# Storing a decoder layer's output from POOL in two indirect transfers that leave out the rows of the last expert

## The chip, the cores and the metric

The kernel runs on one core of one Trainium2 chip. The metric is the device time of one execution in microseconds; the median over several runs is compared.

## The reference

One layer of a decoder trunk on a sequence of T = 256 tokens of D = 2048 float32 values. A token mixer comes first (gMLP, with two large projections), and then a hierarchical mixture of 32 experts, of which every token takes two. The result is normed once more:

```
h = x + chunked_gmlp(rmsnorm(x, norm_mix), ...)
h = h + hier_moe(rmsnorm(h, norm_ffn), ...)      # 32 experts, top 2 of one group of 8
return rmsnorm(h, norm_final)                    # (1, 256, 2048) float32
# an expert: (silu(x @ w_gate) * (x @ w_up)) @ w_down, 2048 -> 512 -> 2048
```

Every expert's weights are three matrices of 4 MB, all of which are read from HBM, whichever tokens come to it.

## The kernel before

The tokens lie in two tiles of 128 (t = 0, 1) with the token on the partition. `acc[:, t, :]` holds the running sum of the layer, one row of 2048 floats (8 KB) per token.

**The experts.** Each expert works on at most CAP = 32 slots, that is on up to 32 tokens gathered by a matmul with a selection matrix. Then follow gate and up (L1564), a transpose of the result (L1641), down (L1662) and a scatter back to tokens (L1675) that DVE adds to `acc` (L1158). SyncE (SP) issues the loads of weights on its own queue, in the order of the experts, as soon as buffers are free. The last expert's down matrix comes in three transfers: the first half in one of 2 MB (L368), the second half in two of 1 MB (L479), each of one row of 8 KB per partition. The last four matmuls wait for the very last of them by `last_in`.

**The last expert is treated apart.** All 256 tokens are finished as if the last expert (number 31) did not exist, while its weights are still on their way. DVE adds expert 30 to `acc` (`add_before_last`, L1204 and L1208), ACT sums the squares (L824), and DVE multiplies by the norm in four instructions of 128x1024 (L1220), two per tile t, each counting up `out_ready`. SP then stores tile t in one transfer of 1 MB when `out_ready` has reached 2 (t + 1):

```
            for t in range(NT):
                sp.wait_ge(out_ready, 2 * (t + 1))
                sp.dma_start(out[0, t * P:(t + 1) * P, :], acc[:, t, :]).then_inc(out_stored, 16)
```

The rows of the last expert's 32 slots are made a second time. `place_tokens` computes for each token its slot (`place`, below 32 for those that have one). Tokens that were routed to expert 31 have their rank as slot, and the slots left over are filled with other tokens, so that exactly 32 tokens have a slot. PE gathers their row numbers (`slot_row`, L1699) and their rows of `acc` (L1704). After the last down matmul DVE adds the expert's output (L1301), ACT and PE make the sum of squares (L877, L1724), and DVE writes the normed rows (L1308, `rows_ready`). They lie as 128 pieces of 512 floats (4 quarters of 32 rows). POOL writes them over the rows stored before by one indirect transfer of 0.26 MB (L581). Since the same rows of `out` were already written by the bulk stores, POOL waits for these first:

```
            pool.wait_ge(slots_ready, 1)
            pool.wait_ge(rows_ready, 1)
            pool.wait_ge(out_stored, 16 * NT)
            pool.indirect_dma_start(...)
```

POOL's queue has other work before that: the loads of the mixer's norm rows (`g_ln`, `b_ln`, 8 KB per partition each) and, during expert 30, four loads of a piece of `norm_final` (L575). SP ends with waits on `out_stored` and `rows_stored`.

Of the kernel before, what the change touches and what calls it, by code (L numbers as in the profile page):

```python
# [10 lines left out]
ALU = mybir.AluOpType  # L11
# [3 lines left out]
P = 128  # L15
EPS = 1e-6
CAP = 32
# [3 lines left out]
def hybrid_layer(nc, x, norm_mix, norm_ffn, norm_final, w_in, ln_g, ln_b, w_s, b_s, w_out,  # L21
                 r_w_group, r_b_group, r_w_exp, r_b_exp, e_gate, e_up, e_down, out):
    _, T, D = x.shape
    NT = T // P
    KD = D // P
# [35 lines left out]
    with ExitStack() as ctx:  # L61
        def sem(name):
            return ctx.enter_context(nc.semaphore(name))

        def sb(name, shape, dt=F32, stack=ctx):
            return stack.enter_context(nc.sbuf_tensor(name, shape, dt))
# [59 lines left out]
        pass_e_i = sb("pass_e_i", [P, MAXX], I32)  # L126
        pass_rank = sb("pass_rank", [P, MAXX])
        pass_t = sb("pass_t", [P, MAXX])
# [15 lines left out]
        token, token_row, quarter = top[:, 0, 0:NT], top[:, 0, NT:2 * NT], top[:, 0, 4:5]  # L144
        place, place_free = top[:, 1, 0:NT], top[:, 1, NT:2 * NT]
        slot_row = pass_e_i[:, 0:1]

# [15 lines left out]
        acc = sb("acc", [P, NT, D])  # L165
# [17 lines left out]
        def xlo(k, n=1):  # L183
# [70 lines left out]
        ones_row_ready, g_ready, tokens_ready, out_ready = (  # L254
            sem("ones_row_ready"), sem("g_ready"), sem("tokens_ready"), sem("out_ready"))
        place_step, same_slot_ready, hot_ready, slots_ps, slots_ready = (
            sem("place_step"), sem("same_slot_ready"), sem("hot_ready"), sem("slots_ps"), sem("slots_ready"))
# [4 lines left out]
        rms_o_done, rstd_o_done, out_stored = sem("rms_o_done"), sem("rstd_o_done"), sem("out_stored")  # L262
# [63 lines left out]
        def chunk_at(i):  # L326
            return buffer_of(i), len(earlier[i])
# [32 lines left out]
        def _(sp):  # L360
# [106 lines left out]
            for e in range(LAST_LOOP, NEXP):  # L467
# [9 lines left out]
                else:  # L477
                    for b in range(2):
                        sp.dma_start(chunk_tile(i)[:, b, :], expert_chunk(i)[:, b, :]  # L479
                                     ).then_inc((chunk_in[chunk_at(i)[0]], last_in)[b], 16)  # L480
            for t in range(NT):
                sp.wait_ge(out_ready, 2 * (t + 1))
                sp.dma_start(out[0, t * P:(t + 1) * P, :], acc[:, t, :]).then_inc(out_stored, 16)
            sp.wait_ge(out_stored, 16 * NT)
            sp.wait_ge(rows_stored, 16)

# [2 lines left out]
        def _(pool):  # L489
# [84 lines left out]
            for j in range(NB):  # L574
                pool.dma_start(g_quarters[j * CAP:j * CAP + 1, :],  # L575
                               norm_final[j * NBLK:(j + 1) * NBLK].rearrange("(a n) -> a n", a=1)).then_inc(final_in, 16)

            pool.wait_ge(slots_ready, 1)
            pool.wait_ge(rows_ready, 1)
            pool.wait_ge(out_stored, 16 * NT)  # L580
            pool.indirect_dma_start(out[0].rearrange("t (j n) -> (t j) n", n=NBLK),  # L581
                                    bass.IndirectOffsetOnAxis(ap=slot_row, axis=0), slot_rows, None
                                    ).then_inc(rows_stored, 16)
# [299 lines left out]
        def _(dve):  # L883
# [276 lines left out]
            def expert(e):  # L1160
                if 0 < e < NEXP - 1:
                    add_out(e - 1, 0)
                if e == NEXP - 1:
                    dve.wait_ge(scatT_ready, NEXP)
                    add_before_last()
                make_hT(e)
                if e + 1 < NEXP:
                    scale_xeT(e + 1)
                if e + 2 < NEXP:
                    choose(e + 2)  # L1170
                if e == NEXP - 2:
                    place_tokens()
                    dve.wait_ge(scat_ps, NEXP)
                    for t in range(NT):
                        ins = dve.tensor_scalar(last_hot[:, t, :, :], iota_cap[:, :].unsqueeze(1).to_broadcast([P, NQ, CAP]),
                                                place[:, t:t + 1], None, ALU.is_equal)
                    ins.then_inc(hot_ready, 1)
                if 0 < e < NEXP - 1:
                    add_out(e - 1, 1)

            def place_tokens():
                rank = rank_of[:, :, NEXP - 1]
                dve.wait_ge(tokens_ready, 2 + NB)
                dve.scalar_tensor_tensor(out=place_free, in0=rank, scalar=-1.0, in1=token, op0=ALU.mult, op1=ALU.add
                                         ).then_inc(place_step, 1)
                dve.wait_ge(place_step, 1)
                dve.tensor_scalar(place_free, place_free, count_f[:, NEXP - 1:NEXP], 1000.0, ALU.add, ALU.add
                                  ).then_inc(place_step, 1)
                dve.wait_ge(place_step, 2)
                dve.tensor_tensor(place, place_free, rank, ALU.min).then_inc(place_step, 1)  # L1190
                dve.wait_ge(place_step, 3)

            def add_before_last():
                dve.wait_ge(gu_half, NEXP - 1)
                dve.tensor_reduce(fold, ident[:, :].rearrange("p (q c) -> p c q", q=NQ), AX_X, ALU.add).then_inc(place_step, 1)
                dve.wait_ge(place_step, 4)
                dve.tensor_copy(same_slot.rearrange("p (q c) -> p q c", q=NQ), fold.unsqueeze(1).to_broadcast([P, NQ, CAP])
                                ).then_inc(same_slot_ready, 1)
                dve.tensor_reduce(slot_weight, scatT[:, (NEXP - 1) % 2, :, :].rearrange("p t m -> p (t m)"), AX_X, ALU.add
                                  ).then_inc(weight_ready, 1)  # L1200
                for j in (2, 3):
                    dve.wait_ge(seed_ps, NB + j + 1)
                    cols = slice(j * NBLK, (j + 1) * NBLK)
                    dve.tensor_tensor(acc[:, 1, cols], FINAL[1][j][:, :], acc[:, 1, cols], ALU.add).then_inc(seed_done, 1)  # L1204
                for t, j, banks in SEEDED:
                    cols = slice(j * NBLK, (j + 2) * NBLK)
                    dve.wait_ge(seed_ps, NB * t + j + 2)
                    dve.tensor_tensor(acc[:, t, cols], banks, acc[:, t, cols], ALU.add).then_inc(seed_done, 1)  # L1208
                dve.wait_ge(slots_ps, 1)
                dve.tensor_tensor(slot_row, SLOT_ROW, quarter, ALU.add).then_inc(slots_ready, 1)  # L1210
                dve.wait_ge(slots_ps, 2)
                dve.tensor_copy(acc_slots, Y[:, :]).then_inc(slots_ready, 1)
                dve.wait_ge(rms_o_done, 1)
                dve.reciprocal(rstd_o, rms_o).then_inc(rstd_o_done, 1)
                dve.wait_ge(rstd_o_done, 1)
                dve.wait_ge(g_ready, 1)
                for t in range(NT):
                    for j in (0, 2):
                        cols = slice(j * NBLK, (j + 2) * NBLK)
                        dve.scalar_tensor_tensor(out=acc[:, t, cols], in0=acc[:, t, cols], scalar=rstd_o[:, t:t + 1],  # L1220
                                                 in1=G_FINAL[:, cols], op0=ALU.mult, op1=ALU.mult).then_inc(out_ready, 1)
# [629 lines left out]
```

## Time and profile before

| | |
|---|---|
| median of 3 runs | 1199.13 us (1198.53 to 1200.3) |
| the profiled execution | 1199.87 us, span 1198.1 us |
| PE busy, share of the span | 885.2 us, 74% |
| DVE / ACT / POOL busy | 380.9 / 232.1 / 23.0 us |
| HBM read / written | 458.05 MB / 2.36 MB, 384 GB/s over the span |
| chain that ended last | DMA 49%, PE 46% |

The span is the time between the first and the last instruction; the execution's own time has 1.8 us around it. The chain that ended last is followed back from the last instruction, at each step to what released it. The first quarter of the span is the mixer, in which PE is busy almost without a break; in the rest the 16 DMA engines are busy for over 90% of each slice, and move 423 to 434 GB/s until the last slice.

### The profile page before, as it was taken

To read this page: it belongs to the slowest core of one execution; us is meant where nothing else is said; L and a number is where in the kernel's file an instruction comes from. 1 tells how busy PE (TensorE), PEld (TensorE's weight loads), DVE (VectorE), ACT (ScalarE), POOL (GpSimd) and SP (SyncE) were. 2 spreads that over 40 slices of the span, in tenths; PEclk is the share of its full clock that TensorE was granted. 3 is DMA by queue.
4 is the path that set the end of the run, shared out by engine and by line. 5 is a ranking of instruction groups with operands and counts; after the bars stand their busy time and mean duration, and the time that the engine had idled before them with its cause. 6 is when DMAs were issued, how large, how long until landed. Compare 5 with 4: busy or idle time off the path is not lost.

```text
span 1198.1 us, 17564 instructions
## 1 busy us (share of the span) xinstructions
PE 885.2 (74%) x7809; PEld 502.3 (42%) x7809; DVE 380.9 (32%) x490; ACT 232.1 (19%) x390; POOL 23.0 (2%) x66
## 2 busy tenths in 40 slices
PE   9999999999984666666666666666666666666676
PEld 7788888877431222223232222322222222222232
DVE  5454866445232222222222222222222222222233
ACT  6544655434210000000000000000000000000003
POOL 1200000000200000000000000000000000000000
PEclk9999999999997777777787877878787878787788
DMA  8875567878999999999999999999999999999997
GB/s 278 321 262 188 190 229 250 298 265 306 396 423 434 428 432 432 429 433 433 429 433 433 430 432 433 430 432 432 430 433 432 430 433 430 433 430 432 427 427 337
DMA packets 47397, 460.93 MB, mean 385 GB/s; under 512 B 3992, under 2 KB 4608, under 8 KB 31744
## 3 DMA queue, kind: packets, MB, share of 16 engines
q1 hardware_dynamic: 46416, 457.19, 92.5%
q0 software_dynamic: 864, 3.21, 0.8%
q8 instruction: 24, 0.39, 0.1%
q14 instruction: 13, 0.11, 0.0%
q10 hardware_dynamic: 80, 0.02, 0.0%
HBM read 458.05 MB, written 2.36 MB: 384 GB/s over the span
## 4 chain that ended last, share of the span: by engine, by line
DMA 49%; PE 46%; ACT 2%; DVE 1%; SPq 1%; issue 1%; POOLq 0%; POOL 0%; ACTq 0%; DVEq 0%
DMA low_slots<-in_e_w_up 45%; PE scattered_out L1354 20%; PE bank L1564 13%; PE bank L1662 5%; PE pair L1525 3%; DMA high_slots<-in_e_w_up 2%; PE scattered_out L1675 1%; PE pair L1533 1%; DMA out_h<-acc 1%; DMA w_raw<-in_a_w_in 1%; ACT arena L776 1%; PE scattered_out L1316 0%; SPq L449 0%; DVE w_lo L889 0%; DVE acc L1220 0%
## 5 line engine op out<-in xcount | busy, mean ns | idle before, releaser
L1158 DVE TENSOR_TENSOR acc<-scattered_out,acc 128x2048 f32<-128x2048 f32 x58 | 132.9, 2291 | 617.4 <-PE scattered_out L1675 617.4
L1564 PE MATMUL bank<-low_slots,arena 128*32 128x256 f32 x2048 | 154.8, 458 | 146.4 <-DMA low_slots<-in_e_w_up 145.9
L1564 PE MATMUL bank<-high_slots,arena 128*32 128x256 f32 x1952 | 145.1, 454 | 137.7 <-DMA high_slots<-in_e_w_up 137.6
L1564 PEld LDWEIGHTS bank<-low_slots,arena 128*32 128x32 f32 x2048 | 83.1, 127 | 219.4 <-issue 188.9
L1564 PEld LDWEIGHTS bank<-high_slots,arena 128*32 128x32 f32 x1952 | 79.5, 126 | 204.6 <-issue 174.6
L889 DVE TENSOR_TENSOR w_lo<-w_raw,w_hi 128x1024 fp32r<-128x1024 f32 x95 | 116.4, 1225 | 114.6 <-ACT w_hi L597 114.1
L597 ACT CAST w_hi<-w_raw 128x1024 fp32r<-128x1024 f32 x95 | 100.2, 1054 | 127.1 <-PE scattered_out L1354 120.4
L1354 PE MATMUL scattered_out<-w_hi,xT_second 128*128 128x512 f32 x376 | 121.3, 394 | 0.2 <-DVE w_lo L889 0.2
L1354 PE MATMUL scattered_out<-w_hi,xT_first 128*128 128x512 f32 x376 | 120.4, 393 | 1.1 <-DVE w_lo L889 1.1
L792 ACT COPY arena<-bank 128x256 f32<-128x256 f32 x32 | 11.9, 373 | 546.2 <-PE bank L1564 546.2
L1662 PE MATMUL bank<-down_slots,arena 128*32 128x512 f32 x944 | 107.9, 595 | 2.1 <-DMA down_slots<-in_e_w_down 1.4
L1354 PEld LDWEIGHTS scattered_out<-w_hi,xT_first 128*128 128x128 f32 x376 | 70.6, 188 | 18.4 <-DVE w_lo L889 1.6
L1354 PEld LDWEIGHTS scattered_out<-w_hi,xT_second 128*128 128x128 f32 x376 | 70.6, 188 | 17.8 <-DVE w_lo L889 0.9
L1354 PE MATMUL scattered_out<-w_lo,xT_second 128*128 128x512 f32 x188 | 73.5, 391 | 0.0
L1354 PE MATMUL scattered_out<-w_lo,xT_first 128*128 128x512 f32 x188 | 73.4, 390 | 0.0
L1675 PE MATMUL scattered_out<-arena 32*128 32x512 f32 x480 | 68.4, 640 | 0.0
L1525 PE MATMUL pair<-h,arena 128*32 128x512 f32 x496 | 59.7, 598 | 0.0
L1662 PEld LDWEIGHTS bank<-down_slots,arena 128*32 128x32 f32 x944 | 27.3, 109 | 60.3 <-issue 56.5
L803 ACT COPY arena<-bank 128x512 f32<-128x512 f32 x31 | 18.2, 587 | 170.1 <-PE scattered_out L1675 162.5
L1354 PEld LDWEIGHTS scattered_out<-w_lo,xT_second 128*128 128x128 f32 x188 | 35.4, 188 | 6.3
L1354 PEld LDWEIGHTS scattered_out<-w_lo,xT_first 128*128 128x128 f32 x188 | 35.3, 188 | 6.1
L1675 PEld LDWEIGHTS scattered_out<-arena 32*128 32x128 f32 x480 | 18.7, 182 | 37.5 <-issue 37.5
(271 smaller groups left out, 514.9 us busy)
## 6 DMA issues: line engine op xcount, KB each, us to landing
down_slots<-in_e_w_down SPq DMA_DIRECT2D x26, 4096.0 KB, 21.1
low_slots<-in_e_w_gate SPq DMA_DIRECT2D x13, 4096.0 KB, 30.5
low_slots<-in_e_w_up SPq DMA_DIRECT2D x13, 4096.0 KB, 39.4
high_slots<-in_e_w_gate SPq DMA_DIRECT2D x13, 4096.0 KB, 30.5
high_slots<-in_e_w_up SPq DMA_DIRECT2D x13, 4096.0 KB, 39.7
w_raw<-in_a_w_in SPq DMA_DIRECT2D x64, 512.0 KB, 3.7
w_raw<-in_a_w_out SPq DMA_DIRECT2D x32, 512.0 KB, 4.8
down_slots<-in_e_w_down SPq DMA_DIRECT2D x6, 2048.0 KB, 18.9
```

Source lines behind the costliest of these rows:

```text
L597: act.copy(w_hi[:, hc % 2, :, :], w_raw[:, hc % 4, :, :]).then_inc(hi_done, 1)
L776: act.copy(xe, XE[:, :]).then_inc(xe_ready, 1)
L792: act.copy(gu, GU[:, 0:256]).then_inc(gu_ready, 1)
L803: act.copy(y_sb, Y[:, :]).then_inc(y_ready, 1)
L889: dve.tensor_tensor(w_lo[:, hc % 2, :, :], w_raw[:, hc % 4, :, :], w_hi[:, hc % 2, :, :].bitcast(F32), ALU.subtract).then_inc(lo_done, 1)
L1158: dve.tensor_tensor(acc[:, t, :], OUT[:, :], (acc if e else h)[:, t, :], ALU.add).then_inc(acc_done, 1)
L1354: ins = pe.matmul(Z[parity][t][:, :], a(k)[:, toks], b[:, hc % 2, j, :], start=(k == 0 and part == 0), stop=(k == KD - 1 and part == 2))
L1525: ins = pe.matmul(XE[j * CAP:(j + 1) * CAP, :], sel[:, e % 2, t, :], gather_columns(t, j), start=(t == 0), stop=(t == NT - 1))
L1533: ins = pe.transpose(TRX[:, b * P:(b + 1) * P], xe.rearrange("p (c k) -> p k c", k=KC)[:, b, :], ident[:, :])
L1564: ins = pe.matmul(GU[c * CAP:(c + 1) * CAP, 0:256], rows_k, gate_columns(rows_of[c // 2][k], c % 2), start=(a == 0 and k == 0), stop=(a == ...
L1662: ins = pe.matmul(Y[j * CAP:(j + 1) * CAP, :], hT[:, b, c * CAP:(c + 1) * CAP], tile[b][:, j * NBLK:(j + 1) * NBLK], start=(c == 0 and b = ...
L1675: ins = pe.matmul(O[j], scatT[rows_j, e % 2, t, :], y_sb[rows_j, :], start=True, stop=True)
```

## The change

The two bulk stores go from SP to POOL and become indirect transfers: each row of `acc` goes to the row number in `kept_row[:, t]`. DVE makes these numbers in `place_tokens` with two more instructions on 128x2 elements: `in_slot` is 512 for a token that has a slot and 0 otherwise, and `kept_row = in_slot + token`. A number above T - 1 = 255 is out of bounds, and the row is left out, without an error. So the bulk stores write 224 rows and the slot rows' transfer the other 32. No row is written twice, and the slot rows' transfer does not wait for `out_stored` any more. `pass_e_i` and `pass_t`, in which the numbers lie, are lists for the extra passes, whose work is over by then.

```diff
+        kept_row, in_slot = pass_e_i[:, 2:2 + NT], pass_t[:, 0:NT]
...
-            for t in range(NT):
-                sp.wait_ge(out_ready, 2 * (t + 1))
-                sp.dma_start(out[0, t * P:(t + 1) * P, :], acc[:, t, :]).then_inc(out_stored, 16)
             sp.wait_ge(out_stored, 16 * NT)
             sp.wait_ge(rows_stored, 16)
...
+            pool.wait_ge(place_step, 5)
+            for t in range(NT):
+                pool.wait_ge(out_ready, 2 * (t + 1))
+                pool.indirect_dma_start(out[0], bass.IndirectOffsetOnAxis(ap=kept_row[:, t:t + 1], axis=0), acc[:, t, :], None,
+                                        bounds_check=T - 1, oob_is_err=False).then_inc(out_stored, 16)
+
             pool.wait_ge(slots_ready, 1)
             pool.wait_ge(rows_ready, 1)
-            pool.wait_ge(out_stored, 16 * NT)
             pool.indirect_dma_start(out[0].rearrange("t (j n) -> (t j) n", n=NBLK),
...
                 dve.wait_ge(place_step, 3)
+                dve.tensor_scalar(in_slot, place, float(CAP), float(2 * T), ALU.is_lt, ALU.mult).then_inc(place_step, 1)
+                dve.wait_ge(place_step, 4)
+                dve.tensor_tensor(kept_row, in_slot, token, ALU.add).then_inc(place_step, 1)
...
-                dve.wait_ge(place_step, 4)
+                dve.wait_ge(place_step, 6)
```

The end of SP's program before (`down_slots` holds the last down matrix, `out_h` is the output in HBM):

```order
138 L368 DMA down_slots<-in_e_w_down 128x4096 [waits y_half]
139 L479 DMA down_slots<-in_e_w_down 128x2048 [waits y_ps]
140 L479 DMA down_slots<-in_e_w_down 128x2048
141 L483 DMA out_h<-acc 128x2048 [waits out_ready] x2
142 L61 UNCONDITIONAL_BRANCH [waits rows_stored,out_stored]
```

With the change the row with L483 is gone from SP, and nothing else on it has moved. The end of POOL's program before:

```order
60 L573 MEMSET low_slots 128x128 [waits gu_half,tokens_ready]
61 L575 DMA low_slots<-in_norm_final 1x16x32 x4
62 L581 DMA out_h<-arena,pass_e_i 1024x512 [waits out_stored,rows_ready,slots_ready]
63 L61 UNCONDITIONAL_BRANCH
```

and with the change:

```order
60 L571 MEMSET low_slots 128x128 [waits gu_half,tokens_ready]
61 L573 DMA low_slots<-in_norm_final 1x16x32 x4
62 L579 DMA out_h<-acc,pass_e_i 256x2048 [waits out_ready,place_step]
63 L579 DMA out_h<-acc,pass_e_i 256x2048 [waits out_ready]
64 L584 DMA out_h<-arena,pass_e_i 1024x512 [waits rows_ready,slots_ready]
65 L61 UNCONDITIONAL_BRANCH
```

The two stores stand on POOL between the loads of `norm_final` and the slot rows' transfer, which has lost its wait on `out_stored`. On DVE, at the end of expert 30, with the change (`arena` is here `last_hot`, the slots' one-hot matrices):

```order
429 L1193 TENSOR_TENSOR top<-top,rank_of 128x2 [waits place_step]
430 L1195 TENSOR_SCALAR pass_t<-top 128x2 [waits place_step]
431 L1197 TENSOR_TENSOR pass_e_i<-pass_t,top 128x2 [waits place_step]
432 L1178 TENSOR_SCALAR arena<-iota_cap,top 128x128 [waits scat_ps]
433 L1178 TENSOR_SCALAR arena<-iota_cap,top 128x128
434 L1161 TENSOR_TENSOR acc<-scattered_out,acc 128x2048 [waits scattered]
```

The second and third of these are new, and stand ahead of `last_hot` and of the add of expert 29's second tile.

## Rows read from the trace of the kernel before

**Rows 1.** The chain of waits in its last 17 us: start, duration, what
```profile
1181.70 11.92 DMA out_h<-acc
...
1194.27 1.31 POOLq L61
```

**Rows 2.** Timeline, 1160 to 1198 us: start, duration, instruction, idle before it
```profile
1160.59 0.23 DVE L1187 TENSOR_SCALAR top<-top,count_f 128x2 f32<-128x2 f32 x1
1160.85 0.16 DVE L1190 TENSOR_TENSOR top<-top,rank_of 128x2 f32<-128x2 f32 x1
...
1161.44 2.28 DVE L1158 TENSOR_TENSOR acc<-scattered_out,acc 128x2048 f32<-128x2048 f32 x1
...
1165.41 0.70 PE L1688 MATMUL pair<-arena 32*128 32x512 f32 x2 [0.80 <-ACT arena L803]
...
1167.49 1.29 DVE L1204 TENSOR_TENSOR acc<-bank,acc 128x512 f32<-128x512 f32 x2 [2.89 <-PE bank L1688]
...
1176.81 4.86 DVE L1220 SCALAR_TENSOR_TENSOR acc<-acc,rows,scattered_out 128x1024 f32<-128x1024 f32 x4
...
1179.32 2.73 SPq L483 DMA_DIRECT2D out_h<-acc  x2
...
1188.75 1.07 PE L1662 MATMUL bank<-down_slots,arena 128*32 128x512 f32 x8 [1.37 <-DMA down_slots<-in_e_w_down]
...
1191.54 0.56 PE L1724 MATMUL pair<-v_mean_var,low_slots 128*128 128x1 f32 x2 [1.72 <-ACT low_slots L877]
...
1192.63 0.75 DVE L1308 SCALAR_TENSOR_TENSOR arena<-arena,v_stats,pair 128x512 f32<-128x512 f32 x1
1194.52 1.07 POOL L581 DMA_INDIRECT out_h<-arena,pass_e_i  x1 [48.15 <-DMA out_h<-acc]
```

**Rows 3.** DMA queues, 1182 to 1188 us: packets, MB, share of the 16 engines
```profile
q1 hardware_dynamic: 336, 2.51, 100.3%
```

**Rows 4.** DMA queues, 1150 to 1151 us, while the norm_final loads run
```profile
q1 hardware_dynamic: 30, 0.43, 99.7%
q0 software_dynamic: 30, 0.00, 2.0%
```

**Rows 5.** DMA queues, 34 to 39 us, while g_ln and b_ln load
```profile
q0 software_dynamic: 230, 1.75, 84.9%
q1 hardware_dynamic: 153, 0.28, 15.7%
```

**Rows 6.** POOL's issue of the norm_final loads, and its queue from 1148 to 1150 us
```profile
1144.28 2.09 POOL L575 DMA_DIRECT2D low_slots<-in_norm_final  x4 [0.28 <-issue]
...
q0 software_dynamic: 55, 0.00, 2.0%
```

**Rows 7.** DMA queue and issue of the slot rows' transfer, 1194 to 1198.1 us
```profile
q0 software_dynamic: 80, 0.26, 15.7%
...
out_h<-arena,pass_e_i POOLq DMA_INDIRECT x1, 2.8
```

**Rows 8.** Windows: PE, PEld, DVE, ACT, POOL busy; granted clock, DMA share, GB/s
```profile
1188.00:1190.00 2.00, 1.07 (x8) 0.16 (x8) 0.11 (x1) 0.00 (x0) 0.00 (x0) 1.00 0.95 401
1190.00:1191.00 1.00, 0.00 (x0) 0.00 (x0) 0.64 (x1) 0.33 (x1) 0.00 (x0) 1.00 0.76 320
1191.00:1192.00 1.00, 0.46 (x2) 0.49 (x2) 0.00 (x0) 0.40 (x2) 0.00 (x0) 0.58 0.49 205
...
1194.00:1196.00 2.00, 0.00 (x0) 0.00 (x0) 0.00 (x0) 0.00 (x0) 1.07 (x1) 0.50 0.00 0
1196.00:1198.10 2.10, 0.00 (x0) 0.00 (x0) 0.00 (x0) 0.00 (x0) 0.00 (x0) 0.50 0.31 125
```

**Rows 9.** The gate and up matmuls (L1564) alone, in two windows
```profile
1120.30:1125.60 5.30, 5.29 (x52) 2.80 (x56) 0.50 0.99 427
1169.20:1173.00 3.80, 3.78 (x64) 2.35 (x64) 1.00 0.99 423
```

## The prediction

> **What bounds the kernel now.** I read the chain of waits first, from its end. It ends in DMA out_h<-acc, from 1181.70 to 1193.62 us, and then in POOL's last transfer [rows 1]. So the removed wait is the one that decides, and the change aims at the right place. The question is what stands behind it. The timeline tells: DVE finishes the slot rows (L1308) at 1192.63 + 0.75 = 1193.38 us, only 0.24 us before the stores have landed [rows 1, 2]. And that second path starts from another transfer: the last eight down matmuls (L1662) begin at 1188.75 us, when the last piece of the down matrix has come in [rows 2]. From there the path is a plain chain of PE, DVE and ACT to 1193.38, which takes 4.63 us.
>
> The third view is the DMA queues. From 1182 to 1188 us SP's queue (q1) alone keeps the 16 engines at 100.3% [rows 3]. There is no free bandwidth before 1188 us, so each byte that is stored earlier pushes a byte of weights back. SP issues its stores from 1179.32 us on, 9.4 us before the last weights are used, but behind them on the same queue. The last weights land at about 1188.73 us and the second store 4.89 us later, at 1193.62 [rows 1, 2]. That is what 2 MB at some 430 GB/s take: the stores come after the weights, on the slowest of the 16 engines at least, and cost them next to nothing. This order is what the change gives up.
>
> **The change, step by step.**
>
> 1. The wait on the stores goes. With the slot rows ready at 1193.38 in place of 1193.62 the end moves by **-0.24 us**. All that follows the release stays: 0.90 us until POOL begins [1193.62 to 1194.52, rows 1, 2], 1.07 us for the instruction, 2.8 us from issue to landing [rows 7], to the span's end at 1198.1. This is the whole gain that there is to have. It holds as long as the slot rows are not late.
>
> 2. DVE gets two instructions on 128x2 elements, 0.23 + 0.16 = 0.39 us by their neighbours L1187 and L1190 [rows 2]. Behind them stands the add of expert 29 (L1158), which ends at 1163.72; PE's next user of it (L1688) starts at 1165.41 and is released by ACT. 1.7 us are free, and DVE then sits idle for 2.89 us before L1204 [rows 2]. Cost 0; without that cover it would be 0.39 us. `last_hot`, made right after them, is used over 10 us later.
>
> 3. SP loses two issues, behind which nothing stands but the final waits: 0.
>
> 4. POOL gets two issues. The first is released when DVE's second L1220 ends, at 1176.81 + 4.86 / 2 = 1179.24 us, and the second at 1181.67 [rows 2]. Each takes 1.07 us if 128 rows cost what 128 pieces cost in L581. The trace has no indirect transfer with rows of 8 KB; the bounds are 1.07 us (price per row) and 4 x 1.07 = 4.3 us (price per byte). I take 1.07, since both have 128 rows. By either, POOL is free at 1190 us at the latest, before the slot rows need it.
>
> 5. **The stores move to another queue, and this is what costs.** When does their first packet move? The slot rows' transfer began at 1194.52, and no byte moved before 1196 [rows 2, 8]: at least 1.5 us. The norm_final loads, on engines full of weights, were issued from 1144.28 and have their first packets between 1148 and 1150 [rows 6]: at least 3.7 us. The first store is issued at 1179.24 + 0.90 = 1180.14, so its first packet moves between 1181.6 and 1183.9 us. At that time the slowest engine has 7.1 to 4.8 us of weights left (to 1188.73).
>
>    Does POOL's queue wait behind SP's? No: from 1150 to 1151 us, with q1 at 99.7%, q1 moves 30 packets and q0 30 [rows 4]. The engines take the queues in turn, packet by packet. The same shows in the bytes from 34 to 39 us: q0 with rows of 8 KB has 84.9% of the engines and q1 15.7% [rows 5]. The weights to come (two transfers of 1 MB with rows of 8 KB) have packets as large as the stores', so in turns the stores get half. An engine has 16 store packets in 4.89 us (2 MB over 16 engines in rows of 8 KB), 0.31 us each. Of these 1 in 8 falls away (32 of 256 rows), which leaves 14. With 4.8 us of weights left, or 15 packets, all 14 store packets still get a turn ahead of the last weight packet. So the last weights come later by 4.89 x 7/8 = **+4.28 us**. The bounds are 0 (q0 served last, or too late) and 4.89 (no row of the slowest engine left out). I take 4.28, because both bounds of the start lead to it.
>
>    On the packets' size, rows 5 have 1.75 MB in 230 packets, 7.6 KB on average with the small ones among them, so an 8 KB row goes as one packet. The Trainium skill, "DMA: Bandwidth & Descriptors", section "SWDGE vs HWDGE vs iDMA", says that a packet should rather have at most 4096 B. By the trace the sum below is 5.1 us, by that rule 3.5 us (third rival).
>
> 6. **PE's clock.** The last 8 matmuls take 1.07 us at a granted clock of 1.00, that is 2.4 GHz [rows 2, 8]. But the clock falls to 0.5 (1.2 GHz) between 1191 and 1192 us, after a stretch in which PE had little to do but these eight [rows 8]. With the change the last piece comes at about 1193.0 and the one before it about 3 us later than now, so PE has the same little bursts with longer gaps, and the last eight run after the fall. L1564 takes 5.29 / 52 = 0.102 us per matmul at 0.50 and 3.78 / 64 = 0.059 at 1.00 [rows 9], a factor of 1.7; the bound by the clock is 2. At 2 the eight take 2.14, at 1.7 1.84. I take **+1.07 us**, since these matmuls have no other wait among them; the other end is 0, where the clock holds on. L1724 at 1191.54 ran at the lower clock already, so it costs nothing more.
>
> Sum: -0.24 + 4.28 + 1.07 = +5.11 us. Against the profiled execution (1199.87 us) that gives 1204.98. It was 0.74 us above the median of the runs, 1199.13; the forecast goes by the median: **1204.2 us**.
>
> **The rivals.**
>
> First rival, not slower: the stores do not push the weights back. That takes a first packet on the slowest engine after 1188.73, or a queue q0 that only gets what q1 leaves. The stores then land about 4.3 us later, at 1193.0, the slot rows are ready at 1193.38, and the end moves by -0.24: 1198.9 us, which is within the 0.2% (2.4 us) that a measurement of this kernel can tell from no change. For it: SP's own stores now do just that, with no loss. Against it: rows 4 and 5 show turns, and POOL would have to be late by 8.6 us after 1180.14, where 3.7 us are the most that I found. It decides from a delay of 5.5 us on: then 3.1 us of weights are left, half of which is a term of 1.6, and the sum is under 2.4 us. I give it 0.12.
>
> Second rival: POOL's issue goes by bytes, 4.3 us each. The first store is then ready at 1184.4 and the second at 1188.7, and only the first one's 7 packets have a turn before the weights end: -0.24 + 2.14 + 1.07 = +3.0, that is 1202.1 us. Against it, 128 rows each. Chance 0.06.
>
> Third rival: the stores go in packets of 4 KB. Rows 7 have 0.26 MB in 80 packets, 16 of them for the semaphore, so 4 KB each; but there two pieces of 2 KB are in a packet, and rows 5 speak against a limit. Each turn would then give 0.155 us to the stores against 0.31 us to the weights. In 4.8 to 7.1 us of weights, the earliest in larger packets, there are 15 to 19 turns, 2.4 to 3.0 us: -0.24 + 2.7 + 1.07 = +3.5, that is 1202.7 us. The rest of the stores lands behind the weights but ahead of the slot rows. The Trainium skill's sentence above is this rule. Chance 0.15.
>
> Fourth rival: the row numbers do not take effect, or out-of-bounds rows cost an engine as much as others. Then the term is 4.89: 1204.8 us, inside the forecast's own range.
>
> A gain of more than 2.4 us would need weights that come earlier than now, and nothing in the change does that. I leave 0.02 for what I do not see.
>
> **How the numbers follow.** The forecast with its own bounds (clock held or not, 14 or 16 packets: +4.0 to +5.7, and half a microsecond around it) has 0.65, from 1202.6 to 1205.4. The second and third rival have 0.21, the first 0.12, the unseen gain 0.02. Slower by over 0.2%: 0.65 + 0.21 is 0.86, less 0.02 for a partial delay under 2.4 us, 0.84. Within 0.2%: 0.14. Faster: 0.02. The range takes in the second and third rival and ends below at 1200.9, short of the first; above it goes to 1206.0, for a POOL that is a microsecond late at the end.
>
> **What the changed profile would show.** Two store issues on POOL at about 1180.1 and 1182.6, of 1.1 us each. From 1182 to 1192 us q0 and q1 with a similar number of packets each. The last eight down matmuls at about 1193.0 in place of 1188.75, at a granted clock of 0.5, taking about 2 us. L1308 ending at about 1198.7, and POOL's last transfer released by it, with the chain of waits going through the last down load and no longer through out_h<-acc. If instead those matmuls still start near 1188.8, step 5 is wrong; if they start between 1190.5 and 1192, the turns are unequal (third rival) or POOL was late (second). If they take 1.07 us, step 6 is wrong.

## The result, and the profile after

| | before | changed |
|---|---|---|
| median | 1198.99 us (12 runs, 1197.95 to 1200.3) | 1202.33 us (12 runs, 1200.62 to 1203.74) |
| ratio | | 1.0028, 95% interval 1.002 to 1.0035 |
| profiled execution | 1199.87 us, span 1198.1 us | 1202.47 us, span 1200.7 us |

The changed kernel is 3.3 us slower: a small difference, but clear of the noise. The forecast was 5.1 us slower, 1204.2 us, with a range from 1200.9 to 1206.0.

The chain of waits of the changed kernel, at its end, tells what took the place of the wait that went (start, duration, what; to compare with [rows 1]):

```profile
1165.26 25.57 DMA down_slots<-in_e_w_down
1190.83 0.04 issue
1190.87 1.98 PE bank L1668 x8
...
1195.62 0.76 DVE arena L1314
...
1196.92 1.19 POOLq L61
```

It no longer goes through out_h<-acc but through the last load of the down matrix, which lands at 1190.83 us. Before, its matmuls began at 1188.75 [rows 2]. The timeline of the changed kernel over the same stretch (lines have moved by three to six, L1564 is now L1570, L1662 is L1668, L1308 is L1314):

```profile
1161.27 0.17 DVE L1195 TENSOR_SCALAR pass_t<-top 128x2 f32<-128x2 f32 x1
...
1161.47 0.16 DVE L1197 TENSOR_TENSOR pass_e_i<-pass_t,top 128x2 int32<-128x2 f32 x1
...
1165.63 0.70 PE L1694 MATMUL pair<-arena 32*128 32x512 f32 x2 [0.80 <-ACT arena L806]
...
1177.03 4.86 DVE L1226 SCALAR_TENSOR_TENSOR acc<-acc,rows,scattered_out 128x1024 f32<-128x1024 f32 x4
...
1178.39 3.84 PE L1570 MATMUL bank<-high_slots,arena 128*32 128x256 f32 x64
1180.46 1.11 POOL L579 DMA_INDIRECT out_h<-acc,pass_e_i  x1 [34.81 <-DVE acc L1226]
...
1182.69 0.99 POOL L579 DMA_INDIRECT out_h<-acc,pass_e_i  x1 [1.12 <-DVE acc L1226]
...
1186.28 1.07 PE L1668 MATMUL bank<-down_slots,arena 128*32 128x512 f32 x8 [0.43 <-DMA down_slots<-in_e_w_down]
...
1190.87 1.94 PE L1668 MATMUL bank<-down_slots,arena 128*32 128x512 f32 x8 [3.53 <-DMA down_slots<-in_e_w_down]
...
1195.62 0.75 DVE L1314 SCALAR_TENSOR_TENSOR arena<-arena,v_stats,pair 128x512 f32<-128x512 f32 x1
1197.14 0.97 POOL L584 DMA_INDIRECT out_h<-arena,pass_e_i  x1 [13.45 <-DVE arena L1314]
```

Three things are to be seen. POOL issues the stores at 1180.46 and 1182.69, 1.11 and 0.99 us each. The last eight down matmuls start at 1190.87 and take 1.94 us in place of 1.07. The last transfer is released by DVE's L1314, as was meant.

For the shift of the weights a measure is needed that does not move when a whole execution is half a microsecond earlier or later at this place. I take the distance from the end of the last gate and up matmul to the start of the last eight down matmuls. Before it is 1188.75 - (1179.02 + 3.89) = 5.84 us, with the matmuls of L1564 from the timeline of before:

```profile
1179.02 3.89 PE L1564 MATMUL bank<-high_slots,arena 128*32 128x256 f32 x64
```

With the change it is 1190.87 - (1178.39 + 3.84) = 8.64 us: the weights are **2.80 us** later. With the 0.87 us of the slower matmuls and -0.24 us for the wait that is gone that makes 3.43 us, and the medians differ by 3.34. (The two profiled spans differ by only 2.6 us, since in the changed kernel's execution the gate and up product ended 0.68 us earlier, and POOL's last transfer began 0.77 us after its release and took 0.97 us, where it was 0.90 and 1.07 us before.)

The DMA queues of the changed kernel, one line per queue (packets, MB, share of the 16 engines), from 1182 to 1184.3 us:

```profile
q1 hardware_dynamic: 124, 0.93, 97.6%
```

and from 1184.3 to 1185:

```profile
DMA packets 51, 0.29 MB, mean 421 GB/s; under 512 B 15, under 2 KB 15, under 8 KB 15
...
q1 hardware_dynamic: 24, 0.15, 50.8%
q0 software_dynamic: 27, 0.15, 50.7%
```

Up to 1184.3 us POOL's queue (q0) moves nothing, though its first store was issued at 1180.46. Then the two share the engines by halves at once, packet for packet. Of the 51 packets 15 are under 512 B; the other 36 carry the 0.29 MB, 8 KB each, and both queues moved 0.15 MB, so the stores' packets are as large as the weights'. The stores do not slow a packet down either: in the trace a weight packet of 8 KB takes 0.31 us (median) before the first store packet and after it.

One more view is needed further on, the queues from 1190.1 to 1190.8 us:

```profile
q0 software_dynamic: 17, 0.13, 44.2%
q1 hardware_dynamic: 1, 0.00, 0.1%
```

The weights' queue carries no row any more, but one small packet, and yet the last eight matmuls start only at 1190.87 us. The trace has the last weight packet's end at 1190.03: from there to the matmuls are 0.84 us.

### The profile page after: what moved, and what is told of

Its sections match the earlier page's. It is cut to its first block, busy times and chain, and to the rows that moved or that the text cites. A ratio compares the mean times of both kernels' runs of the same rounds, so it can differ in the third digit from the quotient of the medians.

```text
span 1200.7 us, 17568 instructions
## 1 busy us (share of the span) xinstructions
PE 886.9 (74%) x7809; PEld 502.3 (42%) x7809; DVE 381.4 (32%) x492; ACT 231.5 (19%) x390; POOL 25.0 (2%) x68
## 4 chain that ended last, share of the span: by engine, by line
DMA 50%; PE 46%; ACT 1%; SPq 1%; DVE 1%; issue 1%; POOLq 0%; ACTq 0%; DVEq 0%
DMA low_slots<-in_e_w_up 45%; PE scattered_out L1360 20%; PE bank L1570 13%; PE bank L1668 5%; PE pair L1531 3%; DMA high_slots<-in_e_w_up 2%; DMA down_slots<-in_e_w_down 2%; PE scattered_out L1681 1%; PE pair L1539 1%; DMA w_raw<-in_a_w_in 1%; ACT arena L779 1%; SPq L450 0%; SPq L466 0%; DMA arena<-in_a_b_s 0%; DVE w_lo L892 0%
## 5 line engine op out<-in xcount | busy, mean ns | idle before, releaser
L1570 PE MATMUL bank<-low_slots,arena 128*32 128x256 f32 x2048 | 154.7, 458 | 145.2 <-DMA low_slots<-in_e_w_up 144.7
L1570 PE MATMUL bank<-high_slots,arena 128*32 128x256 f32 x1952 | 146.1, 456 | 137.8 <-DMA high_slots<-in_e_w_up 137.7
L1570 PEld LDWEIGHTS bank<-low_slots,arena 128*32 128x32 f32 x2048 | 84.3, 127 | 217.1 <-issue 187.4
L1570 PEld LDWEIGHTS bank<-high_slots,arena 128*32 128x32 f32 x1952 | 79.0, 126 | 207.0 <-issue 176.5
L1668 PE MATMUL bank<-down_slots,arena 128*32 128x512 f32 x944 | 109.0, 599 | 4.7 <-DMA down_slots<-in_e_w_down 4.0
L1668 PEld LDWEIGHTS bank<-down_slots,arena 128*32 128x32 f32 x944 | 27.3, 110 | 63.2 <-issue 56.5
```

Source lines behind the costliest of these rows:

```text
L1570: ins = pe.matmul(GU[c * CAP:(c + 1) * CAP, 0:256], rows_k, gate_columns(rows_of[c // 2][k], c % 2), start=(a == 0 and k == 0), stop=(a == ...
L1668: ins = pe.matmul(Y[j * CAP:(j + 1) * CAP, :], hT[:, b, c * CAP:(c + 1) * CAP], tile[b][:, j * NBLK:(j + 1) * NBLK], start=(c == 0 and b = ...
```

## The experiments

All times are compared with runs of the kernel before on the same chip. "Shift" is the distance just defined, less the 5.84 us of before.

**Queue or form: plain stores from POOL.** The kernel before, with this edit:

```diff
-            for t in range(NT):
-                sp.wait_ge(out_ready, 2 * (t + 1))
-                sp.dma_start(out[0, t * P:(t + 1) * P, :], acc[:, t, :]).then_inc(out_stored, 16)
...
+            for t in range(NT):
+                pool.wait_ge(out_ready, 2 * (t + 1))
+                pool.dma_start(out[0, t * P:(t + 1) * P, :], acc[:, t, :]).then_inc(out_stored, 16)
             pool.wait_ge(slots_ready, 1)
```

> Kernel before, but POOL issues the two 1 MB stores as plain transfers of all 256 rows; the slot rows' transfer still waits for them. If the queue is the cost (POOL's queue takes turns with the weights'), the last eight down matmuls start 2 to 3.5 us later than before and the time is 3 to 5 us above before, as with the change or a little more, since no row is left out. If the indirect form or its bounds check is the cost, the time is that of before, within 1 us.

Measured: 1203.74 us against 1198.54, ratio 1.0044 (1.003 to 1.0058). From its timeline:

```profile
1177.33 3.83 PE L1564 MATMUL bank<-high_slots,arena 128*32 128x256 f32 x64
1177.92 0.56 POOL L577 DMA_DIRECT2D out_h<-acc  x1 [33.23 <-DVE acc L1220]
...
1191.97 1.94 PE L1662 MATMUL bank<-down_slots,arena 128*32 128x512 f32 x8 [3.84 <-DMA down_slots<-in_e_w_down]
```

The shift is 1191.97 - 1181.16 - 5.84 = 4.97 us, more than expected, and 4.89 us is what 2 MB take. The cost is the queue, and not the time of the issue: SP issued the same stores at 1179.32 us, 3.6 us before the end of the gate and up matmuls, and POOL 3.2 us before it. The indirect form is not needed for the cost, and is the milder one. Why milder, the last experiments tell.

**The wait alone.** The kernel before, without the wait, and with the slot rows in a DRAM tensor of their own, so that nothing is written twice (the 32 rows of the output stay without the last expert):

```diff
-            pool.wait_ge(out_stored, 16 * NT)
-            pool.indirect_dma_start(out[0].rearrange("t (j n) -> (t j) n", n=NBLK),
+            pool.indirect_dma_start(slot_out[0].rearrange("t (j n) -> (t j) n", n=NBLK),
```

> Kernel before, but the slot rows go to a DRAM tensor of their own and their transfer no longer waits for the stores, which stay on SP's queue (so 32 rows of the output keep the values without the last expert). This is the removal of the wait alone. My theory: 0.2 to 0.3 us less than before, below what can be measured; last eight down matmuls still at about 1188.7 us. A rival in which the wait was worth more than the two paths' difference: over 1 us less.

Measured: 1198.18 us against 1198.54, ratio 1.0 (0.9991 to 1.0009), shift 0.05 us. The best that removing the wait can give is below what can be measured, since the slot rows are ready just when the stores land.

**Holding the stores back.** The changed kernel, with one wait ahead of the two stores on POOL, in one run for the last gate and up product, in the other for the first half of the last down product:

```diff
             pool.wait_ge(place_step, 5)
+            pool.wait_ge(gu_ps, NEXP)        # in the other run: pool.wait_ge(y_half, NEXP)
             for t in range(NT):
```

> The changed kernel, with POOL's stores held until the last gate and up matmul (about 1182.3 us in place of 1179.5). Theory of turns: the first store packet moves about 1186.5 us, with at most 2 us of weights left on the slowest engine, so the down matmuls start 0.5 to 1 us later than before; with the clock term (0 to 0.9 us) the time is 0.3 to 1.7 us above before. Rival, a fixed price of POOL's indirect stores: still 3.3 us above before.

> The changed kernel, with POOL's stores held until the first half of the last down product (about 1185.9 us). Theory of turns: first store packet at about 1189 us, after the last weights, which come as before (1188.7); the stores land by about 1194 and the slot rows go right behind them: between 0.3 us less and 0.5 us more than before. Rival of a fixed price: 3.3 us above before.

Measured: 1198.52 us for the first, ratio 0.9999 (0.999 to 1.0008), and 1198.16 for the second, ratio 0.9997 (0.9988 to 1.0006), against 1198.54. Each has the same two stores, the same bounds check and the same missing wait as the changed kernel; only the start differs. From the timeline of the first:

```profile
1178.85 3.86 PE L1571 MATMUL bank<-high_slots,arena 128*32 128x256 f32 x64
1183.70 1.11 POOL L580 DMA_INDIRECT out_h<-acc,pass_e_i  x1 [37.44 <-PE bank L1571]
...
1188.98 1.07 PE L1669 MATMUL bank<-down_slots,arena 128*32 128x512 f32 x8 [1.79 <-DMA down_slots<-in_e_w_down]
```

and of the second:

```profile
1177.68 3.85 PE L1571 MATMUL bank<-high_slots,arena 128*32 128x256 f32 x64
...
1186.14 1.11 POOL L580 DMA_INDIRECT out_h<-acc,pass_e_i  x1 [41.01 <-PE bank L1669]
1187.42 1.06 PE L1669 MATMUL bank<-down_slots,arena 128*32 128x512 f32 x8 [1.40 <-DMA down_slots<-in_e_w_down]
```

The shifts are 0.43 and 0.05 us, and the last eight matmuls take 1.07 us again. This settles the fixed price: there is none that can be measured. The first of the two came out below what I expected (0.5 to 1 us of shift, 0.3 to 1.7 us of time): stores issued 3 us later cost nothing measurable. Its first store packet moved at 1185.40 us, when weights were still on their way, but the slowest engine can have served only one or two store packets (0.43 us) ahead of its last weights.

**The clock.** The changed kernel, with ten matmuls on constants, into a bank that is free by then, ahead of the wait for the last piece:

```diff
                         if i == NCHUNK - 1 and b == 1:
+                            keep_busy(10, GU)
                             pe.wait_ge(last_in, 32)
```

> The changed kernel with ten bf16 matmuls on constants into a free PSUM bank ahead of PE's wait for the last piece of the down matrix. If the clock is a term of its own, it stays at 1.00 through the last eight down matmuls, which take 1.07 us in place of 1.94, and the time is about 0.9 us under the changed kernel, that is 2.4 us above before. If the clock stays at 0.5 or the term is hidden, no difference from the changed kernel (3.3 above before).

Measured: 1201.65 us against 1198.83, ratio 1.0022 (1.0011 to 1.0032). The two windows of the down matmuls alone (PE busy, PEld busy, granted clock, DMA share, GB/s), first of the changed kernel, for the third and for the last group of eight:

```profile
1186.00:1187.40 1.40, 1.07 (x8) 0.16 (x8) 1.00 1.00 421
1190.80:1192.90 2.10, 1.94 (x8) 0.20 (x8) 0.50 0.18 74
```

and of this experiment:

```profile
1185.90:1187.10 1.20, 1.06 (x8) 0.16 (x8) 1.00 1.00 423
1190.80:1191.90 1.10, 1.07 (x8) 0.16 (x8) 1.00 0.06 22
```

The clock of the last eight is 0.50 (1.2 GHz) with the change, after PE had been idle for 3.53 us before them, and 1.00 (2.4 GHz) where the ten matmuls ran in that gap. The term is 1.94 - 1.07 = 0.87 us, as the trace shows directly. The medians agree in sign (2.8 us above before in place of 3.3, where I expected 2.4), but their intervals overlap, so by time alone it is not shown. This run's shift was 3.67 us, against 2.80, so that not all of the 0.87 shows in the time.

**The wait put back.** The changed kernel with `pool.wait_ge(out_stored, 16 * NT)` restored ahead of the slot rows' transfer.

> The changed kernel with POOL's wait on the stores restored ahead of the slot rows' transfer. The stores have landed by 1192 us and the slot rows are ready at 1196.4, so my theory says: the same as the changed kernel, 3.3 us above before. If the removed wait gave anything back, this one is slower still.

Measured: 1202.07 us, ratio 1.0028 (1.0019 to 1.0037), the same as the changed kernel. The removed wait gave nothing back, for with the change the stores land well before the slot rows are ready. In its profiled execution the last eight matmuls took 1.53 us, at a granted clock of 0.81 at first and of 0.50 then, so the clock's term is not the same 0.87 us in every execution.

**Rows left out or not.** The same, and the factor `float(2 * T)` in `in_slot` is 0.0, so that the indirect stores write all 256 rows, before the slot rows' transfer goes over 32 of them.

> As wait_back, but kept_row is the token's own number for all, so the indirect stores leave out no row (the factor in in_slot is 0). It lies between the changed kernel and the plain stores from POOL: 16 packets on each engine in place of 14, but a start as late as the indirect form's. If the late start limits the shift, the last down matmuls start about as in the changed kernel (2.8 to 3.5 us later than before, by the distance from the last gate and up matmul) and the time is 3.3 to 4 us above before. If the left out rows were what made the shift smaller than 4.9, it is as with the plain stores: 5 us later, and 5 us above before.

Measured: 1202.61 us against 1198.83, ratio 1.0029 (1.002 to 1.0039), shift 1191.71 - 1182.15 - 5.84 = 3.72 us:

```profile
1178.31 3.84 PE L1571 MATMUL bank<-high_slots,arena 128*32 128x256 f32 x64
1179.61 1.11 POOL L579 DMA_INDIRECT out_h<-acc,pass_e_i  x1 [34.13 <-DVE acc L1227]
...
1191.71 1.93 PE L1669 MATMUL bank<-down_slots,arena 128*32 128x512 f32 x8 [3.82 <-DMA down_slots<-in_e_w_down]
```

With all rows stored, the shift is still 1.25 us less than with plain stores. So the left out rows are not the main reason why it is smaller than 4.9. They may be a part: the shift is 0.72 us more than with the wait put back, where the stores were issued 0.4 us later, and a little above the 3.5 that I expected at most; the ratio does not tell the three kernels apart. What a left out row costs the engines can be read from POOL's queue, in the changed kernel from 1182 to 1193 us, and then in this one from 1183.8 to 1192.6:

```profile
q0 software_dynamic: 288, 1.84, 39.7%
```

```profile
q0 software_dynamic: 288, 2.10, 56.4%
```

The number of packets is the same, but 0.26 MB are missing, 32 rows of 8 KB. In the trace each left out row is a packet of 4 B that takes 9 ns.

**One store.** The changed kernel, with tile 0 stored by SP as before, and POOL's last transfer waiting for that one:

```diff
-            for t in range(NT):
+            for t in range(1, NT):
                 pool.wait_ge(out_ready, 2 * (t + 1))
...
+            sp.wait_ge(out_ready, 2)
+            sp.dma_start(out[0, 0:P, :], acc[:, 0, :]).then_inc(x_in[0], 16)
```

> The changed kernel with tile 0 stored by SP as before (POOL's last transfer waits for that store), and only tile 1 by POOL. Its release is 2.4 us later than that of the changed kernel's first store, so by the theory of turns its first packet moves at about 1186.7 us with 1.4 us of weights left on the slowest engine: a shift of 0 to 1.4 us, and 0 to 1.5 us above before (tile 0 may end the chain again). Rival, a price per indirect store: half of 3.3, 1.7 us above before, or more.

Measured: 1199.65 us against 1198.83, ratio 1.0006 (0.9997 to 1.0015), shift 1.11 us:

```profile
1167.80 5.48 PE L1574 MATMUL bank<-high_slots,arena 128*32 128x256 f32 x64 [2.12 <-DMA high_slots<-in_e_w_up]
...
1179.06 3.83 PE L1574 MATMUL bank<-high_slots,arena 128*32 128x256 f32 x64
...
1189.84 1.06 PE L1672 MATMUL bank<-down_slots,arena 128*32 128x512 f32 x8 [2.49 <-DMA down_slots<-in_e_w_down]
```

By the medians this is less than half of the change's 3.4 us, but the interval reaches 1.8 us, so that this run alone does not exclude 1.7 us per store; the two kernels that hold both stores back do. The shift is uncertain here too. The last expert's first gate and up matmuls took 5.48 us, and before 3.83:

```profile
1169.22 3.83 PE L1564 MATMUL bank<-high_slots,arena 128*32 128x256 f32 x64 [1.81 <-DMA high_slots<-in_e_w_up]
```

Counted from the start of this group, which waits for the last load of the up matrix, the last eight down matmuls begin 1189.84 - 1167.80 = 22.04 us later, against 1188.75 - 1169.22 = 19.53 before: a shift of 2.51 us, as much as all of tile 1's packets take on an engine (8 of 0.31 us). In each other run whose group waits for that load the two measures agree within 0.1 us. How much one store costs stays open between 1.11 and 2.51 us in this execution; the time of the median says 0.7.

**Plain stores, later.** The plain stores from POOL once more, but the first one waits for three of DVE's four instructions in place of two (`out_ready` 3).

> As pool_plain (plain stores of all rows from POOL, wait kept), but the first store waits for three of DVE's four instructions in place of two, 1.2 us later, which is about by how much the indirect form's first packet comes later than the plain one's. If the shift is the number of store packets that still get a turn ahead of the last weight packet, the shift falls from 4.97 us to between 3.5 and 4.2 us, like all_rows, and the time is 3.5 to 4.5 us above before in place of 5.2. If the shift is simply the 2 MB, it stays at 4.9.

Measured: 1202.58 us against 1198.83, ratio 1.0025 (1.0014 to 1.0036):

```profile
1178.05 3.86 PE L1564 MATMUL bank<-high_slots,arena 128*32 128x256 f32 x64
1180.60 0.56 POOL L577 DMA_DIRECT2D out_h<-acc  x1 [35.19 <-DVE acc L1220]
...
1190.89 1.94 PE L1662 MATMUL bank<-down_slots,arena 128*32 128x512 f32 x8 [3.82 <-DMA down_slots<-in_e_w_down]
```

The shift is 1190.89 - 1181.91 - 5.84 = 3.14 us, 1.8 us less than for the same stores issued earlier, and somewhat below the 3.5 that I expected at least. In this execution the issue was 1.9 us later against the gate and up product, not 1.2, which fits. All runs with stores on POOL, in the order of the first store's issue:

| kernel | first issue on POOL, us before the last gate and up matmul's end | shift of the last weights, us | time above before, by ratio, us |
|---|---|---|---|
| plain | 3.24 | 4.97 | 5.3 |
| changed, PE kept busy | 2.73 | 3.67 | 2.6 |
| all rows | 2.54 | 3.72 | 3.5 |
| wait put back | 2.14 | 3.00 | 3.4 |
| changed | 1.77 | 2.80 | 3.4 |
| plain, later | 1.31 | 3.14 | 3.0 |
| one store (tile 1) | 0.19 | 1.11 (or 2.51, see above) | 0.7 |
| held to the gate and up product | -0.99 | 0.43 | -0.1 |
| held to the half down product | -4.61 | 0.05 | -0.4 |

(The first two columns come from one execution each, the last from the medians of many.) Apart from the one store, the shift falls with a later start over the whole range, and neither the form of the transfer nor the 32 rows moves a kernel off this trend by more than about half a microsecond.

## Why the prediction was right, and where it was too high

The measured 1202.33 us lies in the stated range, but just below the 1202.6 to 1205.4 to which the forecast's own mechanism was given 0.65. It was caught by the part that was added for the second and third rival, neither of which holds. So the direction and the mechanism are to the prediction's credit, and the hit is in part luck of a wide range. One of its own signs came true as well: the last matmuls started at 1190.87, between 1190.5 and 1192, where it blamed unequal turns or a late POOL. Neither was so, the turns are equal and POOL's instructions took 1.11 and 0.99 us. The stores' first packet was late.

- **Step 1, the wait** (-0.24): right. Alone it is worth nothing that can be measured, and the chain of waits changed hands as described. That all behind the release stays was not quite so: POOL's start and instruction took 0.23 us less.
- **Steps 2 to 4** (nothing): right. DVE's two instructions took 0.17 and 0.16 us, PE's L1694 is still released by ACT (0.80 us, as in [rows 2]), and POOL takes 1.11 and 0.99 us per store, which is the price per row (1.07) and not per byte (4.3). The second rival falls with it.
- **Step 5, the stores push the weights back** (+4.28): the mechanism is right, with turns of one packet each, q0 and q1 at 50.7% and 50.8%. The size was too high: 2.80 us. The sentence that failed is "With 4.8 us of weights left, or 15 packets, all 14 store packets still get a turn". I put the first store packet between 1181.6 and 1183.9 us. It moved at 1184.3, because the indirect store was released at 1179.46 and issued at 1180.46, 1.00 us later and not 0.90, and its first packet came 3.8 us after that, hardly less than the norm_final loads' [rows 6] and far from the idle engines' 1.5. In this execution the last weights would have been used at 1182.23 + 5.84 = 1188.07. So some 3.8 us were left and not 4.8 to 7.1, which would be 12 packets of 0.31 us each. But this counts, as the prediction did, the weights up to the matmuls' start, and the last weight packet ends before it: 0.84 us in the changed kernel, and 0.53 us in the one held to the half down product (1186.89 to 1187.42). That leaves 2.9 to 3.2 us of packets, 9 or 10. The shift of 2.80 us is 9 of them, one store packet for each weight packet that was left. This is an estimate, for the views do not name the single engine, and the first store packet on the slowest may come after the first on any. That the plain stores, issued 1.5 us earlier against the weights, cost the full 4.97 us shows that the sum would have held for an earlier start.
- **Step 6, the clock** (+1.07): right in kind, 0.87 us in size. The matmuls go 1.8 times slower at half the clock, between the two factors that I had (1.7 and 2). The sum took the upper one.
- **Third rival, packets of 4 KB**: it gave 1202.7, close to the measured time, but for a wrong reason. While both queues run each moves 0.15 MB, in packets of 8 KB, so the rows of 8 KB were not split.
- **First rival**: it holds just where it said that it would, for stores issued late. The two kernels that hold the stores back are such cases, and they take 1198.5 and 1198.2 us. The delay from which it decides was worked out wrongly: with 3.1 us of weights left, step 5's own turns give a term of 3.1 us, one store packet for each weight packet, and not half of it. A term of 1.6 us needs a delay of some 7 us in place of 5.5, so the rival was weaker than it was made.
- **Fourth rival**: it falls. The 32 rows are missing from POOL's bytes (1.84 MB against 2.10), and a left out row costs an engine 9 ns.

Of the experiments none is measurably faster than the kernel before. Stores held to the half down product are 0.0003 under it, inside their interval. What they show is that the exact rows and the missing wait are harmless, and that the change loses by its queue and its early start, with the lower clock of the last eight matmuls as what follows from the later weights.

## What to carry to other kernels

In this kernel a store that stood behind loads on one DMA queue cost them nothing that could be measured; the same store on another queue took turns with them, packet for packet. While the DMA engines are full, moving a transfer to another queue is then a decision about priority, and the price falls on whatever waits for the loads: here up to the whole transfer time of the stores (4.97 us), if they start early enough. Before removing a wait that ends the chain, look how far behind the second path is (here 0.24 us), and if the new order has to use another queue, hold it until the loads that matter are through.

## What the runs showed of the hardware that I had not expected

The time from POOL's issue to the first packet depends on what the engines are doing. In the changed kernel it is 3.8 us, with q1 at 97.6%. In the kernel that holds the stores to the half down product, issued at 1186.14, POOL's queue is absent up to 1187.8 us (81 packets of q1 from 1184, at 32.6%), and from 1187.8 to 1188.5 it has this line:

```profile
q0 software_dynamic: 52, 0.31, 107.1%
```

That is 1.7 us, counted from the start of POOL's instruction, which takes 1.11 us itself. In the kernel held to the gate and up product it is also 1.7 us (1183.70 to 1185.40), with q1 at 90.4% in between: some engines had run out of weights by then (q1 is under 100%), so the first packet on any engine says little about the slowest. The Trainium skill, "DMA: Bandwidth & Descriptors", section "Specifications", gives about 1 us to the first byte for this path. The trace agrees in order of size for engines that have run empty, but not for busy ones, where 3.8 us were measured.

An indirect store also reaches the engines later than a plain one. In the changed kernel it begins 1.0 us after its release (DVE's second instruction ends at 1179.46, POOL begins at 1180.46) and takes 1.11 us, against 0.33 us (1177.59 to 1177.92) and 0.56 us for the plain one. Here this lateness was a gain.
